# Value projections' sample rows on four column tiles, bias conversion split into steps, six samples' memory-key sums on ScalarE

## The reference, cut to what matters

```
h = rmsnorm(x);  [q_B | k_B | v_B | u_A | v_A | q_C | gates] = h @ w_in
A: v = layernorm(gelu(z_v)); a = gelu(z_u) * (W_s v + b)
B: window attention, 12 heads of 64; a sample attends to 128 cached rows of each of 3 windows
C: attention over 256 memory rows, 4 heads of 128; each sample has its own cached memory keys
x += (sig(g_A) P_A(A) + sig(g_B) P_B(B) + sig(g_C) P_C(C)) @ w_out
x += MoE(rmsnorm(x)), top 4 of 32 experts, with b_gate_up;  y = rmsnorm(x)
```

## Time and profile before

| | us |
|---|---|
| median of 3 runs | 1443.4 (1442.34 to 1443.64) |
| profiled execution, its own time | 1440.91 |
| its span | 1439.1 |
| PE busy | 1341.8 (93%) |
| DVE busy | 373.6 (26%) |
| ACT busy | 246.8 (17%) |

### The profile page before, as it was taken

The page is one execution under the profiler, slowest core; times in us unless marked ns, Lnnn a source line. Parts: engine busy times, 40 slices in busy tenths (PEclk is TensorE's granted clock), DMA queues, the critical chain, the costliest instruction groups (busy, mean ns, idle before and its releaser), DMA issues.

```text
span 1439.1 us, 19744 instructions
## 1 busy us (share of the span) xinstructions
PE 1341.8 (93%) x7723; PEld 635.6 (44%) x7723; DVE 373.6 (26%) x836; ACT 246.8 (17%) x400; POOL 60.3 (4%) x101
## 2 busy tenths in 40 slices
PE   6999968988899799999999999999999999999995
PEld 5676447655674333343334333433333333333333
DVE  3001684220313422221222222212222122221223
ACT  2000112220203211121111111111111111111112
POOL 2022120210000000000000000000000000000000
PEclk9999989998999899999999999999999999999998
DMA  9998466376993699999999999999999999999993
GB/s 341 364 371 299 164 229 212 111 260 227 330 353 138 235 406 422 422 422 421 422 421 422 423 422 421 423 421 422 422 422 422 422 422 422 422 422 422 422 422 149
DMA packets 84586, 515.13 MB, mean 358 GB/s; under 512 B 8451, under 2 KB 9563, under 8 KB 34608
## 3 DMA queue, kind: packets, MB, share of 16 engines
q1 hardware_dynamic: 77648, 493.69, 84.8%
q0 software_dynamic: 6576, 20.25, 4.3%
q10 hardware_dynamic: 336, 0.82, 0.2%
HBM read 511.21 MB, written 47.52 MB: 388 GB/s over the span
## 4 chain that ended last, share of the span: by engine, by line
PE 64%; DMA 20%; DVE 6%; SPq 5%; issue 2%; ACT 1%; POOL 1%; DVEq 0%; ACTq 0%; POOLq 0%
PE psum L571 61%; DMA weights<-in_w_gate_up 19%; SPq L445 5%; PE psum L574 3%; DVE qk L1357 1%; DMA weights<-in_w_mem_kv 1%; DMA weights<-in_cache_mem_kv 1%; DVE weights L1063 0%; POOL weights L516 0%; DVE pair L1205 0%; DVE weights L1059 0%; DVE samp L1061 0%; DVE samp L1067 0%; ACT th L1505 0%; DVE x L1382 0%
## 5 line engine op out<-in xcount | busy, mean ns | idle before, releaser
L571 PE MATMUL psum<-weights,wsp 128*64 128x512 f32 x2048 | 491.7, 603 | 14.7 <-DMA weights<-in_w_gate_up 14.0
L571 PE MATMUL psum<-weights,merged 128*64 128x512 f32 (+2 forms) x1152 | 272.8, 595 | 1.5 <-issue 1.5
L571 PEld LDWEIGHTS psum<-weights,wsp 128*64 128x64 f32 x2048 | 127.6, 136 | 266.0 <-issue 178.7
L1327 DVE TENSOR_TENSOR hT<-psum,hT 128x264 f32<-128x264 f32 x264 | 101.6, 427 | 527.9 <-PE psum L571 527.8
L571 PE MATMUL psum<-hT,weights 128*128 128x264 f32 x704 | 171.0, 401 | 7.1 <-DVE pair L1205 6.7
L571 PEld LDWEIGHTS psum<-weights,merged 128*64 128x64 f32 (+2 forms) x1152 | 89.6, 140 | 156.4 <-issue 148.7
L571 PEld LDWEIGHTS psum<-hT,weights 128*128 128x128 f32 x704 | 137.9, 198 | 36.1 <-DVE pair L1205 10.4
L1563 ACT COPY bT<-psum 128x264 f32<-128x264 f32 x33 | 12.5, 378 | 483.5 <-PE psum L574 483.5
L571 PE MATMUL psum<-bT,merged 64*128 64x264 f32 x528 | 94.2, 434 | 1.1 <-ACT merged L1582 0.7
L1357 DVE TENSOR_SCALAR qk<-psum,lowest 128x512 f32<-128x512 f32 x64 | 48.0, 751 | 162.4 <-PE psum L571 158.9
L571 PEld LDWEIGHTS psum<-bT,merged 64*128 64x128 f32 x528 | 39.8, 184 | 106.7 <-issue 103.9
(11 more groups left out here) (264 smaller groups left out, 698.1 us busy)
## 6 DMA issues: line engine op xcount, KB each, us to landing
weights<-in_w_gate_up SPq DMA_DIRECT2D x256, 1024.0 KB, 26.1
weights<-in_w_down SPq DMA_DIRECT2D x128, 1024.0 KB, 25.0
out<-in_cache_win_kv SPq DMA_DIRECT2D x8, 4094.0 KB, 25.1
weights<-in_w_in SPq DMA_DIRECT2D x13, 2048.0 KB, 13.6
out<-in_cache_win_kv SPq DMA_DIRECT2D x2, 4088.0 KB, 19.4
weights<-in_cache_mem_kv POOLq DMA_DIRECT2D x14, 512.0 KB, 5.8
weights<-in_cache_win_kv POOLq DMA_DIRECT2D x42, 128.0 KB, 3.9
weights<-in_w_mem_kv SPq DMA_DIRECT2D x2, 2048.0 KB, 18.2
```

Of the source, the lines that this page charges most:

```text
L571: return nc.tensor.matmul(out, lhsT, rhs, start=start, stop=stop, **kw)
L1327: V.tensor_tensor(acc[:, c, :], p_a[j % 2][part], acc[:, c, :], ALU.add).then_inc(s_acc, 1)
```

## The change

1. The steps `v` (2, 0), `v` (2, 1) and `zv` (2) are replaced by `vs`/`vsz` and `zvs`/`zvz`, formed like `wos`/`woz`.
2. In the loop over b the big pieces become: b = 2: zvs and zv 1; b = 3: zvz and zu 0; b = 4, 5, 6: zu 1, zu 2, zu 3; b = 7: none.
3. The products of `sdot` use buffers of their own: `prod_b` for the window keys and two alternating `prod_c` for the memory keys. For samples 0 to 5 the sum of the memory keys in heads goes from DVE to ACT: eight ACTIVATEs (Copy, 128 x 128, with accumulator).
4. The step `bias` becomes four steps, one behind each of the first four pairs of branch b.

```diff
-    s += [("v", t, 0) for t in range(3)] + [("v", t, 1) for t in range(3)]
+    s += [("vs", 0), ("v", 0, 0), ("vsz", 0), ("v", 1, 0), ("vs", 1), ("v", 0, 1), ("vsz", 1), ("v", 1, 1)]
-    big = [("zv", t) for t in range(3)] + [("zu", m) for m in range(4)]
-    s += [("qs", 0), ("qs", 1), ("qcs",), big[0], ("qrest",), ("vts",), ("qlow",), ("selfb",)]
-    big = big[1:]
+    s += [("qs", 0), ("qs", 1), ("qcs",), ("zv", 0), ("qrest",), ("vts",), ("qlow",), ("selfb",)]
+    big = [("zvs",), ("zv", 1), ("zvz",)] + [("zu", m) for m in range(4)]
     for b in range(2, NS):
-        s += [big[b - 2], ("skc", b - 1), ("skb", b), ("sdot", b - 2)]
+        s += {2: big[0:2], 3: big[2:4], 7: []}.get(b, big[b:b + 1]) + [("skc", b - 1), ("skb", b), ("sdot", b - 2)]
         if b == 5:
             s += [("norm_v",)]
...
-        if br == "b":
-            s += [("bias",)]
         for m in range(KD):
             s += [("p", br, m), ("g", br, m)]
+            if br == "b" and m < 4:
+                s += [("bias", m)]
...
PE:
+                elif kind == "vs":
+                    n, = a
+                    w, c = weights(f"v{n}"), (512, 256)[n]
+                    for k in range(KD):
+                        r = slice(k % 4 * E, (k % 4 + 1) * E)
+                        last = mm(o[r, 0:c], hT[:, k, NT - E:NT], w[:, k, 0:c], k < 4, k >= 4)
+                elif kind == "vsz":
+                    n, = a
+                    taken(pe, "vs", n)
+                    c = (512, 256)[n]
+                    last = mm(o[0:NS, 0:c], sample_sum, sample_v[:, n, 0:c])
...
DVE, sdot:
+                    if b >= 2:
+                        dve.wait_ge(s_csum, min(b - 1, BY_ACT))
+                    V.tensor_tensor(prod_c[b % 2].rearrange("p (t c) -> p t c", t=2), kv_c[b % KEYS], ...).then_inc(s_qread, 1)
                     dve.wait_ge(s_qread, 2 * b + 2)
                     dve.sem_inc(s_kv_used, 1)
-                    seq(V.tensor_reduce(sC[:, b * 8:(b + 1) * 8], prod.rearrange("p (h c) -> p h c", c=CD), AX.X, ALU.add))
+                    if b >= BY_ACT:
+                        seq(V.tensor_reduce(sC[:, b * 8:(b + 1) * 8], prod_c[b % 2].rearrange("p (h c) -> p h c", c=CD), AX.X, ALU.add))
...
ACT:
+                elif kind == "sdot":
+                    b, = a
+                    if b < BY_ACT:
+                        act.wait_ge(s_qread, 2 * b + 2)
+                        for i in range(2 * CH):
+                            head = prod_c[b % 2][:, i * CD:(i + 1) * CD]
+                            ins = A.activation(head, head, ACT.Copy, accum_out=sC[:, b * 2 * CH + i:b * 2 * CH + i + 1])
+                        ins.then_inc(s_csum, 1)
...
bias, on ACT (part 0: L1547's cast; 1: L1549's; 2: L1550's) and on DVE (part 0: fills and copies; 1: L1262; 3: L1264):
+                    if part == 0:
+                        act.wait_ge(s_brow_in, 16)
+                        act.wait_ge(s_vaout, 16)
+                        A.copy(bias[0:E, 0:2 * D], brow).then_inc(s_bhi, 1)
+                    elif part == 1:
+                        act.wait_ge(s_bres, 1)
+                        A.copy(flat_qk.bitcast(BF16)[0:E, 0:2 * D], brow).then_inc(s_bmid, 1)
+                    elif part == 2:
+                        A.copy(bias[E:2 * E, 0:2 * D], brow).then_inc(s_bmid, 1)
```

More of the change, by code:

```diff
@@ L52 @@
 ROUND = 2
+BY_ACT = 6
 KEYS = 3
@@ L159, in schedule @@
     return s
[L163 to L167, removed]
+ROTATING = {"vec", "wsp", "rel", "sbias", "memT", "kc", "xT", "vc", "kct", "q", "k", "v", "vs", "vsz", "kt", "qc", "qs", "qcs", "vts",
+            "selfb", "zv", "zvs", "zvz", "zu", "vat", "sp", "p", "g", "ssum", "svb", "svc", "svbt", "svct", "wos", "wo", "woz", "xt", "rt", "lg", "pos"}
+LAST_USE = {("kc", 3): 0, ("vc", 1): 1, ("q", 3): 2, ("k", 1): 3, ("k", 5): 4, ("v", 1, 0): 5, ("v", 1, 1): 6, ("qc", 3): 7,
+            ("zv", 1): 8, ("zu", 3): 9}
 for _n, _br in enumerate("acb"):
@@ L220, in build @@
         q_mid = scratch[0:NS, 4224:4864].bitcast(BF16)
+        prod_b = scratch[:, 6144:6144 + BW]
+        prod_c = [scratch[:, a:a + 1024] for a in (4864, 7168)]
         qs, slf = scratch[0:NS, 4864:6144], prod[0:NS, 0:BW]
@@ L357, in build @@
         s_smix = sem("sample_mix")
+        s_csum = sem("memory_scores_summed")
         s_kvout, s_kvcout, s_vaout = sem("out_kv"), sem("out_memkv"), sem("out_chunk_v")
@@ L537, in _ @@
             pool.dma_start(dst, kvc).then_inc(s_kvcout, 16)
-            taken(pool, "v", 2, 1)
+            taken(pool, "v", 1, 1)
+            taken(pool, "vsz", 0)
+            taken(pool, "vsz", 1)
             taken(pool, "kt", 2, 1)
@@ L669, in _ @@
                 elif kind == "vts":
-                    taken(pe, "v", 2, 1)
+                    taken(pe, "vsz", 0)
+                    taken(pe, "vsz", 1)
                     for i in range(NH // 2):
@@ L690, in _ @@
                     mm(spread_c, pick_b[:, b:b + 1].to_broadcast([PARTS * E, P]), q_parts[:, BW:BW + 512]).then_inc(s_qspreadc, 1)
+                elif kind == "vs":
[9 more added lines that the diff above has]
+                    last = mm(o[0:NS, 0:c], sample_sum, sample_v[:, n, 0:c])
+                elif kind == "zvs":
+                    w = weights("zv")
+                    for k in range(KD):
+                        r = slice(k % 4 * E, (k % 4 + 1) * E)
+                        last = mm(o[r, :], hT[:, k, NT - E:NT], w[:, k, :], k < 4, k >= 4)
+                elif kind == "zvz":
+                    taken(pe, "zvs")
+                    last = mm(o[0:NS, :], sample_sum, sample_v[:, 0, :])
                 elif kind == "zv":
@@ L1108, in _ @@
                     b3 = sB.rearrange("p (b h) -> p b h", b=NS)
+                    dve.wait_ge(s_csum, BY_ACT)
                     seq(V.tensor_scalar(sC, sC, C_SCALE, None, ALU.mult))
@@ L1252, in _ @@
                 elif kind == "bias":
[L1254 to L1264, removed]
+                    part, = a
+                    if part == 0:
+                        dve.wait_ge(s_kvout, 16 * 12)
+                        V.memset(xparts[0:PARTS * E, 0, 2, :], 0.0)
+                        V.memset(small[:, 0:880], 0.0)
+                        V.memset(lowest[0:SLOTS, :], -3.4028234663852886e38)
+                        V.memset(lowest[SLOTS:2 * SLOTS, :], -LIMIT)
+                        V.tensor_copy(before_b[:], before)
+                        V.tensor_copy(ones_b[:], ones[:])
+                    elif part == 1:
+                        dve.wait_ge(s_bhi, 1)
+                        V.tensor_tensor(brow, brow, bias[0:E, 0:2 * D], ALU.subtract).then_inc(s_bres, 1)
+                    elif part == 3:
+                        dve.wait_ge(s_bmid, 2)
+                        V.tensor_tensor(bias[2 * E:3 * E, 0:2 * D], brow, flat_qk.bitcast(BF16)[0:E, 0:2 * D], ALU.subtract).then_inc(s_bias, 1)
                 elif kind == "lg":
@@ L1443, in _ @@
                     take(v_tok[0:tn, t, n2 * 512:n2 * 512 + w], o[0:tn, 0:w], "v")
-                elif kind == "zv":
-                    t, = a
+                elif kind == "vs":
+                    take(sample_v[:, a[0], :], o, "v") if a[0] == 0 else take(sample_v[:, 1, 0:256], o[:, 0:256], "v")
+                elif kind == "vsz":
+                    w = (512, 256)[a[0]]
+                    take(v_tok[0:NS, 2, a[0] * 512:a[0] * 512 + w], o[0:NS, 0:w], "v")
+                elif kind == "zvs":
+                    take(sample_v[:, 0, :], o, "zv")
+                elif kind in ("zv", "zvz"):
+                    t = a[0] if kind == "zv" else 2
                     tn = TILES[t][1]
```

13 lines of the change are left out of this document (8 added, 5 removed).

## The result

The changed kernel took 1429.33 us (median of 5 runs, 1425.11 to 1433.05) against 1443.4 of the kernel before, on the same chip: ratio 0.9901, 95% interval 0.9876 to 0.9925. Repeated on later occasions it gave 1427.31 (ratio 0.9892, interval 0.9869 to 0.9914) and 1427.47 (0.9895, 0.9878 to 0.9912). The forecast was 1428.3, in a range from 1423 to 1433.5.

What follows compares the result with a forecast made beforehand. Experts wait for weights, but their stream starts with the mixer's end, so mixer time (PE, DVE) counts. 6.0 + 1.4 + 7.7 = 15.1 us off 1443.4 gives 1428.3, range 1423 to 1433.5.

Steps and rivals of the forecast that it cites:

- The limit: Experts: their weight stream starts with PE's start on expert 0, so a microsecond of mixer is a microsecond of time.
- Part 1: Value projections: 8-row tiles put on column tiles save 6.0 us, from 5.2 to 6.3.
- Part 3: Branch b: splitting the bias step into steps behind the pairs saves 7.7 us, from 4.5 to 8.7.
- The remaining 1.0: Branch b, behind pair 1: ACT's cast, waiting for DVE's subtraction, delays the next gate; 1.0 us is paid.
- Part 2: Loop over the samples: reordered large pieces and sums moved to ACT save 1.4 us; ends -4.0 and 2.8.
- The new wait: Loop, norm_v: DVE's reciprocal waits for ACT's root, queued behind sample 3's sums; 0.8 us later than before.
- from there everything is the same again: Loop, from vat (about 200.4 against 201.78) up to sample 6 and the attention: durations unchanged.
- the fourth rival: The rival Keys of sample 7 late: zu 3's earlier transfers delay a key load, kernel slower; chance 0.04.
- No stall at the root: Loop: sums finish before DVE wants the root; vat 3.0 earlier, 18.1 us saved in all, 1425.3; chance 0.15.
- Tables reloaded: Loop, ACT: table loads around each sample's sums cost 2.6 a sample; gain 9.9 us, 1433.5; chance 0.17.
- Swallowed by the weights: Experts: weight stream bound from a fixed time, so nothing moves, 1443.4; chance 0.04.
- Keys of sample 7 late: Loop: sample 7's key load, behind a 2 MB block and 4 MB copy, stalls DVE 16.6 us; 1444.9; chance 0.04.

Runs made afterwards that it cites:

- values_bias: The kernel before with the value projections' sample rows on column tiles and the bias in four steps, loop over the samples as before; ratio 0.9909 to before.
- root_first: The changed kernel with ACT taking the square root of norm_v ahead of sample 3's eight sums instead of behind them; 1425.71 us against 1427.31.

## Why the prediction was right

**The limit.** The mixer's microseconds counted, as said: two experts take 59.63 us before and after, and all but 1.7 us of the mixer's gain arrives.

**Part 1, 6.0 us (5.2 to 6.3).** Measured 5.76, in eleven traces. The tiled group of 512 columns with the whole tile behind it is 8.92 where 1.84 + 6.96 = 8.80 was taken; the three groups between the first adding matmul and the second are 116.48 - 104.77 = 11.71 where 6.96 + 1.10 + 3.55 = 11.61 was. ACT's copies lay hidden. The change inserts three tiled groups, not the four that the prediction speaks of; no number hangs on it.

**Part 3, 7.7 us (4.5 to 8.7).** Measured 7.88. The remaining 1.0 is a gap of 0.85, at the pair named, with the engines in the order named: DVE's subtraction, ACT's cast, Tanh, DVE, PE.

**Part 2, 1.4 us (-4.0 to 2.8).** Measured 0.54 by the first pair of traces. Its steps, carried over to the trace after by subtracting the 7.05 us by which the loop starts earlier: first statistics 171.75 forecast, 172.01 measured; reciprocal 178.45 and 178.63; `vat` 193.35 and 193.69; sums of a sample 2.3 and 2.45. The new wait stood where it was put. The Trainium skill (ScalarE: Activation LUTs, Table sets) says copy is in every set; the trace agrees, with 48 sums and no table load between them and a Gelu. The step that was off is "from there everything is the same again": PE, having stood 9.92 us, ran the spatial gating at the lower clock, which the stretch from 190 to 200 us shows (columns as in the earlier trace rows):

```profile
190.00:195.00 5.00, 3.22 (x14) 2.30 (x15) 2.53 (x6) 3.22 (x22) 0.98 (x2) 0.50 1.19 432
195.00:200.00 5.00, 3.36 (x14) 2.89 (x14) 4.14 (x10) 0.00 (x0) 0.00 (x0) 0.50 0.65 155
```

0.50 is 1.2 GHz; before, at `vat`, zu 3 had just run and the clock was full. That is 5.27 instead of 4.77 from `vat` to sample 6. And the term has less under it than it seemed: values_bias, without any of the loop's edits, has the loop at 49.69. The loop of before varies from 50.28 to 51.70 with the clock of its first group, and that of the changed kernel from 48.03 to 49.74 (its first row 8.99 or 10.69 us long). The 1.4 is within this spread. That variation drops out when the loop is read from behind its first group, where PE spreads the next query: from there to sample 6 it is 38.25 to 38.27 us in the five traces of the loop as changed, and 40.85, 40.83, 40.88, 40.58 and 40.27 in the five without the part. Of these 2.0 to 2.6 us the tiled group `zvs`, which now lies ahead of that point, takes 1.8 to 2.0 back. At equal clock the edit is worth 0 to 0.8 us in the loop.

**What was missed.** POOL's wait was in the trace of before, on its chain, and the fourth rival spoke of the very transfers that lengthen it, but as a danger to sample 7's keys. Their earlier release was worth 0.1 to 1.0 us on the other side. PE's wait of 10 to 12 us for the last memory values stands in no part of the prediction either, which names PE or DVE as busy in every stretch it costs; it did no harm, because it moves with the mixer. The keys were late only when the root was moved, by 0.74 us and not 16.6.

**The sum.** 15.1 forecast; medians give 14.1, 15.1 and 14.5 on three occasions. The 16.0 of the two profiled executions is, part by part: 5.76 + 0.54 + 7.88 = 14.2 for the three parts against 15.1; 2.4 in the attention's start (clock and POOL); 1.2 ahead of the value projections, where neither kernel differs (below); less 1.7 at the end and 0.1 for the rest. That the total came so close is in part luck: part 2 and part 1 came out 0.9 and 0.2 short, part 3 0.2 over, and terms that were not forecast filled the gap.

**The rivals.** *No stall at the root*: refuted as it stood (3.29), and root_first shows its price, 2.3 where the working said 3.0. *Tables reloaded*: no load between the sums. *Swallowed by the weights*: the experts kept their pace, and all but 1.7 us arrived. *Keys of sample 7 late*: did not happen.

## What to carry to other kernels

Here two stages whose engine is never idle, or stands for one known step, were costed from rows to 0.3 us, and such edits (whole tiles made into column tiles, a serial conversion cut and laid under its neighbours) arrive in full and add up. Work moved to an idle engine is worth what that engine's next result allows: look for what the receiver still owes the giver, and move that ahead of the new work in the same edit. When a step moves, follow the transfers that it releases in both directions: they may come into the way of something, or out of it.

## What the hardware showed that I had not expected

The granted clock moves stages that no edit touches, by 1.5 to 2.4 us each. The stretch from 70 to 80 us, before the first edit, in the trace of before and in that of after:

```profile
70.00:80.00 10.00, 10.00 (x42) 7.57 (x41) 1.10 (x4) 1.78 (x4) 0.63 (x1) 0.83 1.08 374
```
```profile
70.00:80.00 10.00, 10.00 (x48) 7.43 (x49) 1.38 (x4) 1.78 (x4) 0.63 (x1) 1.00 1.16 416
```

PE is busy all the time in both, the clock is 0.83 in one and full in the other, and from PE's transposes at 29 us to the value projections it is 66.86 us against 65.33. The changed kernel had started them 0.3 later, which leaves the 1.2 above. The clock there is 0.83 in five of the fourteen traces, with edits and without. The first large group of PE (64 instructions from about 15 us on) took 14.05 us in nine traces and 15.8 to 16.3 in the five others, the first attention group 4.26 or 5.8 to 5.95. At the very end the last 24 transposes ran at 0.50 in a part of their time (1408 to 1413 us) after, in one piece before:

```profile
1406.56 2.61 PE L580 MATMUL psum<-sq,hT 128*128 128x128 f32 x11 [3.75 <-issue]
1409.79 3.03 PE L580 MATMUL psum<-sq,hT 128*128 128x128 f32 x13 [0.62 <-issue]
```
```profile
1424.07 4.47 PE L574 MATMUL psum<-sq,hT 128*128 128x128 f32 x24 [3.55 <-issue]
```

This last one may not be chance. From expert 0 to the end the two traces of before have 956.62 and 957.45 us and values_bias 957.06, the eleven others 958.3 to 959.7, and in all nine traces with the loop's part the 24 transposes take 6.1 to 6.4 us from first to last, against 4.3 to 5.4 in the five without. Whether the change brings this about, and how, is open; 1 to 2 us of the gain may be lost there.

Together these are of the size of the spread among runs of one kernel, 1.5 to 8.7 us, and larger than the whole of part 2. A difference of 2 us between two kernels can be read from the stages of their traces, but only among stages of one clock level.
